# A one-core transformer block: in the gate and up projections, one 2x2 block of products per column chunk formed as seven products of sums

## The chip, the cores and the metric

The kernel runs on one core of a Trainium2 chip, in one launch, all in float32. The metric is device time in microseconds (us), the median of several runs. Matmuls run on TensorE (PE) and write to PSUM, which has eight banks of 128 partitions x 512 float32. VectorE (DVE) and ScalarE (ACT) do elementwise work, SyncE (SP) issues the weight loads, and semaphores order the engines.

## The reference

For 256 tokens and D = 2048 it computes a feed-forward layer, a mixer and a second feed-forward layer, each followed by a layer norm. The change touches the first two products of both feed-forward layers:

```python
def swiglu(x, w_gate, w_up, w_down):                  # D = 2048, D_FF = 5632
    return (jax.nn.silu(x @ w_gate) * (x @ w_up)) @ w_down

h = layer_norm(DEEPNORM_ALPHA * h + 0.5 * swiglu(h, ffn1_w_gate[l], ffn1_w_up[l], ffn1_w_down[l]), ...)
mix = hybrid_mixer(h, ...)
h = layer_norm(DEEPNORM_ALPHA * h + mix, ...)
h = layer_norm(DEEPNORM_ALPHA * h + 0.5 * swiglu(h, ffn2_w_gate[l], ffn2_w_up[l], ffn2_w_down[l]), ...)
```

## The kernel before

**Units.** Every weight matrix is streamed in units of 256 rows x 512 columns (512 KB): SP loads a unit into one of eight `raw` slots (L422). To keep float32 precision, each unit is split in two: ACT copies it to a rounded `whi` (`split_hi`, L486), DVE subtracts to get the rest, `wlo` (`split_lo`, L493). There are three split slots. The activations `xT` are kept as the same kind of pair. A product is then three matmuls (hi x hi, hi x lo, lo x hi; L505, L506, L507), each with a 128x128 block of `xT` as weights and 512 columns moving. A unit has two 128-row blocks and is used by two halves of the tokens (t0, t1), so it is 12 matmuls (`token_mm`, `unit_mm`).

**Chunks.** The 5632 gate and up columns are 11 chunks of 512. A chunk is 8 gate units, summed in the two banks `acc0`, and 8 up units, summed in the two banks `acc1`: 192 matmuls. Chunk 0 is written out by hand; chunks 1 to 10 are one loop on each engine (`gate_up` in `ffn_pe`, `ffn_act`, `ffn_dve`, `ffn_loads`). Within a chunk ACT takes tanh of the gate (L1079), DVE turns it into the gate's silu (L1184, `gated`) and, once all up units of the chunk are done, multiplies by `acc1` (`gate_times_up`, L977); PE transposes the result in the next chunk, after its fourth unit (`hT_pe`, L958, 8 small matmuls into `tp`), and ACT and DVE split it into `hT` (L964, L968).

**What sets the order.** All orders are written out by hand, per engine, and engines run their queues in order. Four counters carry the dependences: `raw_loaded` (a slot has landed), `hi_done`, `lo_done` (splits done) and `unit_used` (PE is through with a unit's split). ACT and DVE split `LEAD` = 2 units ahead of PE, so a `split_hi` waits for `unit_used` of the unit that had its slot. SP loads a slot again when `lo_done` says it was split. `Stream` and `ring_place` work out the counts and the slots.

**Seven products, already in use elsewhere.** The down projection (`Pair`, `form_mm`, L1026 to L1028) already computes some 2x2 blocks (two token halves x two units of rows, two column chunks) with seven products P1 to P7 instead of eight. It needs sums of weight blocks (DVE, L1203 to L1218, 128x1024 each), sums of activations (`sumA`), and foldings of the product banks.

Of the kernel before, what the change touches and what calls it, by code (L numbers as in the profile page):

```python
# [19 lines left out]
P = 128  # L20
# [16 lines left out]
class Phase:  # L37


    def __init__(self, name, iters, units, width, raws=None):  # L40
        self.name, self.iters, self.units, self.width = name, iters, units, width
        self.raws = units if raws is None else raws

    def places(self, slots):

        return self.raws if slots == RAW_SLOTS else self.units

# [96 lines left out]
class Stream:  # L144


    def __init__(self, phases):
        self.phases = phases
        self.base = []
        self.loads = []  # L150
        at, loads = 0, [0] * RAW_SLOTS
        for ph in phases:
            self.base.append(at)
            self.loads.append(list(loads))
            at += ph.iters * ph.units
            for s in range(RAW_SLOTS):
                loads[s] += ph.iters * self.uses(ph, s)

    @staticmethod
    def uses(ph, s):  # L160
        return sum(ring_place(u, ph.raws, RAW_SLOTS) == s for u in range(ph.raws))
# [5 lines left out]
    def loaded(self, p, it, u):  # L167

        n = self.phases[p].raws
# [6 lines left out]
    def freed(self, p, it, u, slots):  # L176
# [5 lines left out]
        s = ring_place(u, n, slots)  # L182
        same = [v for v in range(u) if ring_place(v, n, slots) == s]
        if same:
            c = same[-1] + 1
        else:
            prev = [v for v in range(n) if ring_place(v, n, slots) == s]
            c = prev[-1] - n + 1 if prev else -n
            if not over:
                if p > 0:  # L190
                    m = self.phases[p - 1].places(slots)
                    prev = [v for v in range(m) if ring_place(v, m, slots) == s]
# [7 lines left out]
def hybrid_block(nc, x, x_t, ffn1_w_gate, ffn1_w_up, ffn1_w_down, ln1_g, ln1_b, w_in, q_norm_g, kv_norm_g,  # L200
# [40 lines left out]
    F1GU, F1DA, F1DB, WA, WZ, WB, WC, WQI, WUQ, WO, F2GU, F2DA, F2DB = range(13)  # L241
    QI_CHUNKS, UQ_CHUNKS, QU = IH * ID // BANK, AH * AD // BANK, QT // UNIT_KT
    st = Stream([
        Phase("ffn1 gate and up", GATE_CHUNKS, 2 * KU, BANK),
        Phase("ffn1 down: chunks 0 and 1", 1, len(PAIRS[0].items), BANK, len(PAIRS[0].raws)),
        Phase("ffn1 down: chunks 2 and 3", 1, len(PAIRS[1].items), BANK, len(PAIRS[1].raws)),
# [7 lines left out]
        Phase("ffn2 gate and up", GATE_CHUNKS, 2 * KU, BANK),  # L254
        Phase("ffn2 down: chunks 0 and 1", 1, len(PAIRS[0].items), BANK, len(PAIRS[0].raws)),
        Phase("ffn2 down: chunks 2 and 3", 1, len(PAIRS[1].items), BANK, len(PAIRS[1].raws)),
# [9 lines left out]
    with ExitStack() as ctx:  # L266
# [23 lines left out]
        form_sum = mz("form_sum", 88, [P, UNIT_KT, BANK])  # L290
        fourth_hi = mz("fourth_hi", 92, [P, 1, UNIT_KT, BANK], F32R)
# [89 lines left out]
        pinv = at("pinv", cz + 1824, [P, T, AH])  # L381
        alog = at("alog", cz + 1888, [P, BH])
# [34 lines left out]
        def load_unit(sp, p, it, u, src):  # L417
            s = ring_place(u, st.phases[p].units, RAW_SLOTS)
# [10 lines left out]
        def split_place(p, it, u):  # L429

            n = st.phases[p].units
            if p in (F1DB, F2DB) and n - EDGES <= u < n:
                slot = u - n + EDGES
                return edge_hi, edge_lo, slot, st.index(p, 0, edge_free(slot))
            if plan_of(p) is not None:
# [4 lines left out]
                elif s < SPLIT_SLOTS:  # L440
                    last = [v for v in range(2 * KU) if ring_place(v, 2 * KU, SPLIT_SLOTS) == s][-1]
                    free = st.index(GU[f], GATE_CHUNKS - 1, last + 1)
# [30 lines left out]

        def raw_unit(p, u):
# [3 lines left out]
        def split_hi(act, p, it, u):  # L478
            n, w = st.phases[p].units, cut_width(p, it, u)
            hi, _, s, free = split_place(p, it, u)  # L480
            v = raw_unit(p, u)
            r = ring_place(v % st.phases[p].raws, n, RAW_SLOTS)
# [4 lines left out]

        def split_lo(dve, p, it, u):
            n, w = st.phases[p].units, cut_width(p, it, u)
            hi, lo, s, _ = split_place(p, it, u)  # L490
            r = ring_place(raw_unit(p, u) % st.phases[p].raws, n, RAW_SLOTS)
# [4 lines left out]
        def token_mm(pe, p, it, u, acc, half, stat, kt0, first, last):  # L496
# [4 lines left out]
            for k in range(UNIT_KT):  # L501
# [3 lines left out]
                pe.matmul(o, hi, w_hi[:, s, k, 0:width], start=first and k == 0, stop=False)  # L505
                pe.matmul(o, hi, w_lo[:, s, k, 0:width], start=False, stop=False)  # L506
                ins = pe.matmul(o, lo, w_hi[:, s, k, 0:width], start=False, stop=last and k == UNIT_KT - 1)  # L507
# [320 lines left out]
        GU, DOWN = [F1GU, F2GU], [(F1DA, F1DB), (F2DA, F2DB)]  # L828
        EXITS, ENTRIES = (F1DB, WO, F2DB), (WA, F2GU)
# [35 lines left out]
        def ffn_loads(sp, f, w_gate, w_up, w_down, load_x):  # L865
# [4 lines left out]
            def gate_up(c):  # L870
                for v, view in ((0, gate_v), (KU, up_v)):
                    for u in range(KU):
                        load_unit(sp, GU[f], c, v + u, view[:, 2 * u:2 * u + 2, bass.ds(c * BANK, BANK)])
# [8 lines left out]
            with sp.Fori(1, GATE_CHUNKS) as c:  # L882
                gate_up(c)
# [3 lines left out]
            for pair, p in enumerate(DOWN[f]):  # L887
                plan = PAIRS[pair]
                for r, (u, c) in enumerate(plan.raws):
                    s = ring_place(r, len(plan.raws), RAW_SLOTS)  # L890
                    if r < RAW_SLOTS and pair == 0:
                        sp.wait_ge(lo_done, st.freed(p, 0, r, RAW_SLOTS))
                    elif r < RAW_SLOTS:
                        before = max(v for v in range(len(PAIRS[0].raws)) if v % RAW_SLOTS == s)
# [21 lines left out]
        F_STEPS = len(SUM_STEPS) + sum(PAIR_STEPS)  # L916

        def summed(f, step):

            return F_STEPS * f + SUM_STEPS.index(step) + 1  # L920

        def made(f, p, name, q):

            pair = DOWN[f].index(p)
            return F_STEPS * f + len(SUM_STEPS) + sum(PAIR_STEPS[:pair]) + 4 * q + MADE[name]

        def folded(f, pair, n):

            return F_STEPS * f + len(SUM_STEPS) + sum(PAIR_STEPS[:pair]) + 4 * len(PAIRS[pair].quads) + n
# [5 lines left out]
        def sum_act(f, n):  # L935

            return 6 * f + n + 1

        def form_raw(p, i):
# [3 lines left out]
            return raw[:, plan_of(p).raw_of(i) % RAW_SLOTS]  # L943
# [1823 lines left out]
```

## Time and profile before

| | us |
|---|---|
| median of 3 runs | 1924.69 (1923.57 to 1925.12) |
| the profiled execution, its own time | 1924.74 |
| its span, first to last instruction | 1923.0 |
| PE busy | 1903.5 (99%) |
| DVE busy | 1256.1 (65%) |
| ACT busy | 893.1 (46%) |

The two gate and up stages lie at about 6 to 495 us and 1190 to 1680 us of the span, the two down stages behind them, the mixer between 725 and 1190 us. The span is what the trace covers; the time outside it is 1.7 us. "Busy" of PE counts matmuls whose ends are modelled and that overlap, so the spacing of their starts says more than their durations. A row of a timeline gives start, duration, engine, line and operation, and in brackets how long the engine had been idle and what released it.

### The profile page before, as it was taken

How to read it: one execution, taken by the hardware profiler on the slowest of the kernel's cores; microseconds unless marked ns; L12 is line 12 of the kernel's file. 1: busy time of each engine (PE TensorE's matmuls, PEld its weight loads, DVE VectorE, ACT ScalarE, POOL GpSimd, SP SyncE). 2: the span in 40 equal slices, each digit the busy share in tenths (PEclk: the TensorE clock that was granted, in tenths of full speed). 3: DMA queues.
4: the chain of work that ended last, by engine and by line, in shares of the span. 5: the costliest groups of instructions: out<-in, count | busy, mean ns of one | idle time of the engine just before them, and what ended most of it. 6: DMA issues, size and time to landing. Idle time of an engine off the chain costs nothing.

```text
span 1923.0 us, 28047 instructions
## 1 busy us (share of the span) xinstructions
PE 1903.5 (99%) x10490; PEld 1621.3 (84%) x10490; DVE 1256.1 (65%) x1415; ACT 893.1 (46%) x996; POOL 66.9 (3%) x93
## 2 busy tenths in 40 slices
PE   9999999999999999999999999999999999999997
PEld 7888888888888888999999888888888888888886
DVE  5555555455788887667766958554555555588887
ACT  5444444344454553554744534443444444455452
POOL 0000000000000001300131000000000000000000
PEclk9999999999999999999999999999999999999999
DMA  8666666667655575664442067566566666646654
GB/s 305 188 191 189 187 191 185 189 176 238 199 173 200 180 283 155 214 188 150 130 132 89 23 218 252 167 186 190 178 189 189 200 187 191 188 133 214 217 193 186
DMA packets 185366, 357.38 MB, mean 186 GB/s; under 512 B 11328, under 2 KB 23616, under 8 KB 184272
## 3 DMA queue, kind: packets, MB, share of 16 engines
q1 hardware_dynamic: 183600, 347.43, 57.9%
q0 software_dynamic: 1696, 8.99, 1.4%
q8 instruction: 47, 0.77, 0.2%
q14 instruction: 23, 0.19, 0.0%
HBM read 354.28 MB, written 2.10 MB: 185 GB/s over the span
## 4 chain that ended last, share of the span: by engine, by line
PE 90%; DVE 5%; DMA 2%; issue 1%; ACT 1%; POOL 0%; POOLq 0%; DVEq 0%; ACTq 0%
PE acc L505 24%; PE acc L507 24%; PE acc L506 24%; PE acc L528 3%; PE acc L532 3%; PE acc L530 3%; DMA raw<-in_ffn_w_down_dram 2%; PE tp L1026 1%; PE tp L1028 1%; PE tp L1027 1%; PE tp L958 1%; DVE wlo L493 1%; PE acc L1026 1%; PE acc L1028 1%; PE acc L1027 1%
## 5 line engine op out<-in xcount | busy, mean ns | idle before, releaser
L493 DVE TENSOR_TENSOR wlo<-raw,whi 128x1024 fp32r<-128x1024 f32 (+2 forms) x559 | 668.0, 1201 | 576.4 <-ACT whi L486 574.8
L486 ACT ACTIVATE whi<-raw 128x1024 fp32r<-128x1024 f32 (+2 forms) x559 | 575.1, 1036 | 746.2 <-PE acc L507 676.7
L505 PE MATMUL acc<-whi,xT 128*128 128x512 f32 (+2 forms) x1644 | 631.7, 384 | 0.8 <-ACT zab L1662 0.4
L507 PE MATMUL acc<-whi,xT 128*128 128x512 f32 (+2 forms) x1644 | 626.5, 381 | 0.0
L506 PE MATMUL acc<-wlo,xT 128*128 128x512 f32 (+2 forms) x1644 | 625.9, 381 | 0.0
L505 PEld LDWEIGHTS acc<-whi,xT 128*128 128x128 f32 x1644 | 309.0, 188 | 64.5 <-issue 1.8
L507 PEld LDWEIGHTS acc<-whi,xT 128*128 128x128 f32 x1644 | 308.9, 188 | 59.2
L506 PEld LDWEIGHTS acc<-wlo,xT 128*128 128x128 f32 x1644 | 309.1, 188 | 55.7
L505 PE MATMUL acc<-whi,hT 128*128 128x512 f32 x352 | 137.6, 391 | 1.1 <-DVE wlo L493 1.1
L507 PE MATMUL acc<-whi,hT 128*128 128x512 f32 x352 | 137.2, 390 | 0.0
L506 PE MATMUL acc<-wlo,hT 128*128 128x512 f32 x352 | 137.2, 390 | 0.0
L528 PE MATMUL acc<-xT,whi 128*128 128x256 f32 x384 | 108.9, 284 | 0.0
L532 PE MATMUL acc<-xT,wlo 128*128 128x256 f32 x384 | 108.9, 283 | 0.0
L530 PE MATMUL acc<-xT,whi 128*128 128x256 f32 x384 | 108.9, 283 | 0.0
L1098 ACT ACTIVATE whi<-raw 128x1024 fp32r<-128x1024 f32 x54 | 57.4, 1062 | 48.8 <-PE acc L507 16.5
L505 PEld LDWEIGHTS acc<-whi,hT 128*128 128x128 f32 x352 | 66.1, 188 | 15.7 <-issue 1.6
L507 PEld LDWEIGHTS acc<-whi,hT 128*128 128x128 f32 x352 | 66.1, 188 | 13.8
L506 PEld LDWEIGHTS acc<-wlo,hT 128*128 128x128 f32 x352 | 66.1, 188 | 13.6
L530 PEld LDWEIGHTS acc<-xT,whi 128*128 128x128 f32 x384 | 73.9, 192 | 0.0
L532 PEld LDWEIGHTS acc<-xT,wlo 128*128 128x128 f32 x384 | 73.8, 192 | 0.0
L528 PEld LDWEIGHTS acc<-xT,whi 128*128 128x128 f32 x384 | 73.8, 192 | 0.0
L1224 DVE TENSOR_TENSOR wlo<-raw,whi 128x1024 fp32r<-128x1024 f32 x54 | 65.9, 1221 | 4.9 <-ACT whi L1098 4.3
(382 smaller groups left out, 2046.1 us busy)
## 6 DMA issues: line engine op xcount, KB each, us to landing
raw<-in_ffn_w_down_dram SPq DMA_DIRECT2D x176, 512.0 KB, 6.7
raw<-in_ffn_w_up_dram SPq DMA_DIRECT2D x175, 512.0 KB, 3.7
raw<-in_ffn_w_gate_dram SPq DMA_DIRECT2D x174, 512.0 KB, 3.8
raw<-in_w_in_dram SPq DMA_DIRECT2D x48, 512.0 KB, 3.9
raw<-in_w_out_dram SPq DMA_DIRECT2D x32, 512.0 KB, 7.0
raw<-in_w_in_dram SPq DMA_DIRECT2D x32, 260.0 KB, 2.8
raw<-in_w_in_dram SPq DMA_DIRECT2D x16, 456.0 KB, 6.1
raw<-in_w_q_idx_dram SPq DMA_DIRECT2D x8, 512.0 KB, 4.0
```

The costliest lines, as they stand in the source:

```text
L486: act.activation(hi[:, s, :, 0:w], raw[:, r, :, 0:w], ACT.Copy).then_inc(hi_done, 1)
L493: dve.tensor_tensor(lo[:, s, :, 0:w], raw[:, r, :, 0:w], hi[:, s, :, 0:w].bitcast(F32), ALU.subtract).then_inc(lo_done, 1)
L505: pe.matmul(o, hi, w_hi[:, s, k, 0:width], start=first and k == 0, stop=False)
L506: pe.matmul(o, hi, w_lo[:, s, k, 0:width], start=False, stop=False)
L507: ins = pe.matmul(o, lo, w_hi[:, s, k, 0:width], start=False, stop=last and k == UNIT_KT - 1)
L528: pe.matmul(o, whi[:, s, k, cols], hi, start=first and k == 0 and c == 0, stop=False, skip_group_check=True)
L530: pe.matmul(o, whi[:, s, k, cols], lo, start=False, stop=False, skip_group_check=True)
L532: ins = pe.matmul(o, wlo[:, s, k, cols], hi, start=False, stop=end, skip_group_check=True)
L1026: pe.matmul(o, x_hi, w_hi[:, s, k], start=i == touches[0] and k == 0, stop=False)
L1027: pe.matmul(o, x_hi, w_lo[:, s, k], start=False, stop=False)
L1098: act.activation(w_hi[:, s], form_raw(p, i), ACT.Copy).then_inc(hi_done, 1)
L1224: dve.tensor_tensor(w_lo[:, s], form_raw(p, i), w_hi[:, s].bitcast(F32), ALU.subtract)\
```

## The change

The change gives each chunk 2 to 10 of both feed-forward layers one 2x2 block: token halves t0 and t1, row units 6 and 7 (`QUAD_A`, `QUAD_B`), and as its two columns the gate and the up weights of the chunk. With X the activations and G, U the weights, the eight unit-half products of units 6 and 7 (48 matmuls) become seven (42): P1 = X(t0,6) G6, P2 = X(t0,7) G7, and P3 to P7 with sums of weights (DVE, `chunk_add`) and sums of activations (`sumX`, made once per layer, in chunk 1).

P1, P5, P6 and P7 of a chunk are computed at the end of the chunk before it, P2, P3 and P4 at its start. Call g0 to g5 the plain gate units of a chunk and u0 to u5 its plain up units. The new order of a looped chunk c is: g0, P2, g1, P3, g2, P4, g3, g4, g5, u0, u1, then for chunk c+1 P1, u2, P5, P6, u3, P7, and u4, u5 of chunk c. P5 goes to the bank `tp[3]`, P7 to `tp[2]`, P6 and P1 to the halves of `acc0`. Foldings combine them: U2 = P1 + P6, U3 = U2 + P7 (into `acc0[1]`, where P4 and gate units are added), U4 = U2 + P5 (ACT copies it into `acc1[0]` as a seed for P3 and up units), V = U4 + P7 (into `acc1[1]`). Chunk 1 ("lead": 8 gate units and 2 up units, then the 10 items above from u0 on) and chunk 10 ("last", 15 items) are written out, chunks 2 to 9 are the loop. There are four split slots in the loop instead of three, and ACT and DVE run three items ahead (`CHUNK_LEAD`).

```diff
+def chunk_plans(a, b, units):
+    some = [u for u in range(units) if u not in (a, b)]
+    gate, up = plain(0, some), plain(1, some)
+    here = [gate[0], ("P2", 0, 0), gate[1], ("P3", 0, 0), gate[2], ("P4", 0, 0), *gate[3:]]
+    ahead = up[:2]
+    ahead += [("P1", 0, 0), up[2], ("P5", 0, 0), ("P6", 0, 0), up[3], ("P7", 0, 0), *up[4:]]
+    raws_here = [(some[0], 0, 0), (b, 0, 0)] + [(u, 0, 0) for u in some[1:]]
+    u1 = [(u, 1, 0) for u in some]
+    raws_ahead = u1[:2] + [(a, 0, 1), (a, 1, 1), u1[2], (b, 1, 1), *u1[3:]]
+    lead = plain(0, range(units)) + plain(1, (a, b)) + ahead
...
+    body, last = here + ahead, here + up
+    shift = len(here) - 1
...
+            Chunk(body, raws_here + raws_ahead, [(i + (i >= shift)) % 4 for i in range(len(body))]),
...
+        sumX = mz("sumX", 92, [P, 4, UNIT_KT, 2, P], F32R)
+        gate_sum = mz("gate_sum", 80, [P, UNIT_KT, BANK])
+        gate_sum2 = mz("gate_sum2", 84, [P, UNIT_KT, BANK])
...
+        folding = at("folding", cz + 1888, [P, BANK])
```

PE. A product is six matmuls; the waits in front of it:

```diff
+            def chunk_form(p, it, c, i):
...
+                if name in ("P1", "P6"):
+                    half = int(name == "P6")
+                    pe.wait_ge(acc0_free[half], c + (n0[GU[f]] + 1))
+                if name == "P5":
+                    pe.wait_ge(sem("formed"), in_gate(f, "S4 low") if p == G1[f] else in_chunk(f, p, it, "U4"))
+                if name == "P7" and p != G1[f]:
+                    pe.wait_ge(sem("formed"), in_chunk(f, p, it, "V"))
+                if name == "P3":
+                    pe.wait_ge(sem("sum_act"), act_in_chunk(f, p, it, "seed"))
+                pe.wait_ge(lo_done, st.index(p, it, i + 1))
```

SP. When a `raw` slot is free again, as the item whose `split_lo` must be done:

```diff
+            def released(plan, r):
+
+                u, c, ahead = plan.raws[r]
+                if u == QUAD_B and c == 0 and not ahead and ("P4", 0, 0) in plan.items:
+                    return plan.at("P4") - 1
+                if (u, c, ahead) == (QUAD_A, 0, 1):
+                    return plan.at("P1") + 1
+                if (u, c, ahead) == (QUAD_A, 1, 1):
+                    return plan.at("P7")
+                if (u, c, ahead) == (QUAD_B, 1, 1):
+                    return len(plan.items) + CHUNKS[1].at("P3")
+                return plan.at("unit", u, c)
```

ACT and DVE, the loop over a chunk's items:

```diff
+                for i in range(CHUNK_LEAD, n + (LEAD if p == GE[f] else CHUNK_LEAD)):
+                    if i == CHUNK_LEAD and p != G1[f]:
+                        act.wait_ge(sem("formed"), in_chunk(f, p, it, "U4"))
+                        act.wait_ge(acc1_free[0], c + n1[GU[f]])
+                        act.activation(acc1[:, 0], folding[:], ACT.Copy).then_inc(sem("sum_act"), 1)
+                    split_hi(act, p, it, i)
...
+                    if p != GE[f] and i == plan.at("P1") + 4:
...
+                        act.activation(folding[:], acc0[:, 0], ACT.Copy).then_inc(sem("sum_act"), 1)
...
+                gate_times_up(dve, f, c, st.index(p, it, 0))
+                if p != G1[f]:
+                    to_folding(p, it, "U4")
+                    second_up(p, it, c)
+                for i in range(CHUNK_LEAD, n + (LEAD if p == GE[f] else CHUNK_LEAD)):
+                    split_lo(dve, p, it, i)
+                    if p == G1[f]:
+                        x_sums(i)
                     if i == 8:
                         hT_dve(dve, f, c)
+                    if i + 2 < n and plan.items[i + 2][0] in ("P4", "P5", "P6", "P7"):
+                        chunk_add(p, it, plan.items[i + 2][0])
+                    if i == gate_end + 3:
+                        gate_part(c)
+                    if p != GE[f] and i == n:
+                        to_folding(p, it, "U2")
+                    if p != GE[f] and i == n + 1:
+                        to_folding(p, it, "U3")
```

How the order moves. VectorE, at the start of a looped chunk, from its first instruction on (`gated` x `acc1`), before:

```order
L977 TENSOR_TENSOR gated<-gated,acc 128x512 [waits s_acc0a_free,s_unit_used]
L977 TENSOR_TENSOR gated<-gated,acc 128x512 [waits s_acc0b_free]
L492 REGISTER_ALU
L493 TENSOR_TENSOR wlo<-raw,whi 128x1024 [waits s_hi_done]
L492 REGISTER_ALU
L493 TENSOR_TENSOR wlo<-raw,whi 128x1024 [waits s_hi_done]
```

The same place in the changed kernel, from behind those two multiplications (there L1212) on; `folding` holds U2, then U4, `tp` is P5 and then P7, `chunk_lo` is the fourth split slot, `gate_sum` and `gate_sum_62` are the two weight sums:

```order
L1550 TENSOR_TENSOR folding<-tp,folding 128x512 [waits s_formed]
L1554 REGISTER_ALU
L1556 TENSOR_TENSOR acc<-tp,folding 128x512 [waits s_acc1b_free,s_formed]
L1149 REGISTER_ALU
L1150 TENSOR_TENSOR chunk_lo_65<-raw,chunk_hi_64 128x1024 [waits s_hi_done]
L1507 ISA
L1532 REGISTER_ALU [waits s_raw_loaded4]
L1533 REGISTER_ALU [waits s_formed]
L1534 TENSOR_TENSOR gate_sum<-raw,gate_sum_62 128x1024 [waits s_lo_done]
L1149 REGISTER_ALU
L1150 TENSOR_TENSOR wlo<-raw,whi 128x1024 [waits s_hi_done]
```

Between the multiplications and the low split of g2 (the last row) stand U4, V, the low split for P3 and the weight sum for P4; before, the low splits followed the multiplications at once.

TensorE, where up units 5 and 6 met in the loop before; a unit is twelve matmuls, of which the last three and the first three are shown:

```order
L505 MATMUL acc<-whi,xT 128x512
L506 MATMUL acc<-wlo,xT 128x512
L507 MATMUL acc<-whi,xT 128x512
L515 REGISTER_ALU
L505 MATMUL acc<-whi,xT 128x512 [waits s_lo_done]
L506 MATMUL acc<-wlo,xT 128x512
L507 MATMUL acc<-whi,xT 128x512
```

And the end of u2, P5 and the first matmuls of P6 in the loop now:

```order
L631 MATMUL acc<-whi,xT 128x512
L1253 REGISTER_ALU
L1258 REGISTER_ALU [waits s_formed]
L1266 MATMUL tp<-whi,sumX 128x512 [waits s_lo_done]
L1267 MATMUL tp<-wlo,sumX 128x512
L1268 MATMUL tp<-whi,sumX 128x512
L1266 MATMUL tp<-whi,sumX 128x512
L1267 MATMUL tp<-wlo,sumX 128x512
L1268 MATMUL tp<-whi,sumX 128x512
L1258 REGISTER_ALU [waits s_acc0b_free]
L1266 MATMUL acc<-chunk_hi_64,sumX 128x512 [waits s_lo_done]
L1267 MATMUL acc<-chunk_lo_65,sumX 128x512
```

A product takes six matmuls between two waits for a split, where a unit takes twelve, and it has a second wait of its own.

## Rows read from the trace of the kernel before

**Rows 1.** The page: busy time and share of the span by engine; granted clock in tenths

```profile
PE 1903.5 (99%) x10490; PEld 1621.3 (84%) x10490; DVE 1256.1 (65%) x1415; ACT 893.1 (46%) x996; POOL 66.9 (3%) x93
PEclk9999999999999999999999999999999999999999
```

**Rows 2.** Waits: who waited for whom, us in total, times, longest

```profile
ACT whi L486 <- PE acc L507: 676.7, 385, 4.4
DVE wlo L493 <- ACT whi L486: 574.8, 396, 4.7
...
PE acc L505 <- DVE wlo L493: 1.1, 3, 0.4
```

**Rows 3.** Windows: start:end, length, busy and count by engine, clock, DMA share, GB/s

```profile
227.95:272.42 44.47, 44.47 (x201) 36.83 (x200) 23.01 (x21) 18.62 (x18) 0.00 (x0) 1.00 0.65 188
561.00:700.00 139.00, 139.00 (x614) 115.17 (x614) 120.17 (x111) 75.72 (x74) 0.43 (x1) 1.00 0.59 203
```

**Rows 4.** Timeline of TensorE over the start of a chunk, and its transposes

```profile
227.72 0.39 PE L507 MATMUL acc<-whi,xT 128*128 128x512 f32 x1
227.95 0.39 PE L505 MATMUL acc<-whi,xT 128*128 128x512 f32 x1
228.17 0.39 PE L506 MATMUL acc<-wlo,xT 128*128 128x512 f32 x1
228.40 0.39 PE L507 MATMUL acc<-whi,xT 128*128 128x512 f32 x1
228.63 0.39 PE L505 MATMUL acc<-whi,xT 128*128 128x512 f32 x1
...
238.83 1.04 PE L958 MATMUL tp<-ident,gated 128*128 128x128 f32 x8
239.63 0.47 PE L505 MATMUL acc<-whi,xT 128*128 128x512 f32 x1
```

**Rows 5.** Timeline of VectorE and ScalarE, same chunk

```profile
228.15 1.28 DVE L977 TENSOR_TENSOR gated<-gated,acc 128x512 f32<-128x512 f32 x2 [0.40 <-PE acc L507]
229.35 1.22 DVE L493 TENSOR_TENSOR wlo<-raw,whi 128x1024 fp32r<-128x1024 f32 x1
...
257.39 2.36 DVE L493 TENSOR_TENSOR wlo<-raw,whi 128x1024 fp32r<-128x1024 f32 x2 [1.91 <-ACT whi L486]
...
228.15 1.06 ACT L486 ACTIVATE whi<-raw 128x1024 fp32r<-128x1024 f32 x1 [1.66 <-PE acc L507]
```

**Rows 6.** Lines: groups by line, busy us and mean ns, idle before

```profile
L977 DVE TENSOR_TENSOR gated<-gated,acc 128x512 f32<-128x512 f32 x44 | 28.3, 684 | 9.7 <-PE acc L507 9.7
L1218 DVE TENSOR_TENSOR form_sum<-raw 128x1024 f32<-128x1024 f32 x14 | 17.1, 1220 | 0.0
L2151 DVE COPY t<-tp 128x256 f32<-128x256 f32 x10 | 4.1, 423 | 7.4 <-PE tp L2470 7.2
L840 ACT ACTIVATE whi<-raw 128x512 fp32r<-128x512 f32 x6 | 3.8, 632 | 1.1 <-DMA raw<-in_ffn_w_up_dram 0.9
```

**Rows 7.** DMA issues: size and median us to landing

```profile
raw<-in_ffn_w_down_dram SPq DMA_DIRECT2D x176, 512.0 KB, 6.7
raw<-in_ffn_w_up_dram SPq DMA_DIRECT2D x175, 512.0 KB, 3.7
raw<-in_w_out_dram SPq DMA_DIRECT2D x32, 512.0 KB, 7.0
```

**Rows 8.** Landing times of raw in 540:700 (down), then in 230:275 (gate and up)

```profile
DMA to landing us min/median/max: 3.7/7.5/15.4
...
DMA to landing us min/median/max: 3.6/3.7/4.8
```

**Rows 9.** Windows: TensorE busy, clock, DMA share, GB/s, opening and end of down

```profile
0.00:22.00 22.00, 19.68 (x90) 1.00 0.93 338
700.00:740.00 40.00, 38.95 (x184) 1.00 0.88 287
```

More of the change, by code:

```diff
@@ L181, in freed @@
             it, u = it + 1, u - n
-        s = ring_place(u, n, slots)
-        same = [v for v in range(u) if ring_place(v, n, slots) == s]
+        ph = self.phases[p]
+        s = ph.place(u, slots)
+        same = [v for v in range(u) if ph.place(v, slots) == s]
         if same:
@@ L186, in freed @@
         else:
-            prev = [v for v in range(n) if ring_place(v, n, slots) == s]
+            prev = [v for v in range(n) if ph.place(v, slots) == s]
             c = prev[-1] - n + 1 if prev else -n
@@ L253, in hybrid_block @@
         Phase("w_out", OUT_CHUNKS, KU, BANK),
[L254 to L256 removed]
+        *gate_up_phases("ffn2"),
+        *down_phases("ffn2"),
     ])
@@ L440, in split_place @@
                 elif s < SPLIT_SLOTS:
-                    last = [v for v in range(2 * KU) if ring_place(v, 2 * KU, SPLIT_SLOTS) == s][-1]
-                    free = st.index(GU[f], GATE_CHUNKS - 1, last + 1)
+                    last = [v for v, slot in enumerate(CHUNKS[2].slots) if slot == s][-1]
+                    free = st.index(GE[f], 0, last + 1)
                 else:
@@ L996, in ffn_pe, with chunk_unit @@
-            gate_up(0, False)
-            with pe.Fori(1, GATE_CHUNKS) as c:
-                gate_up(c, True)
+            if f == 0:
+                first_units_pe(pe)
+            else:
+                entry_units(pe, 2, F2GU)
+            def chunk_unit(p, it, c, i):
+                plan = chunk_of(p)
+                _, u, kind = plan.items[i]
+                mine = [v for v, item in enumerate(plan.items) if item[0] == "unit" and item[2] == kind]
+                quad = p != G1[f]
+                pe.wait_ge(lo_done, st.index(p, it, i + 1))
+                for half in range(2):
+                    first = i == mine[0]
+                    if first and not quad:
+                        pe.wait_ge((acc0_free, acc1_free)[kind][half], c + (n0, n1)[kind][GU[f]])
+                    elif first and kind == 0 and half == 0:
+                        pe.wait_ge(sem("sum_act"), act_before_chunk(f, p, it, "P1 out"))
+                    elif first and kind == 0:
+                        pe.wait_ge(sem("formed"), before_chunk(f, p, it, "U3"))
+                    elif first and half == 1:
+                        pe.wait_ge(sem("formed"), in_chunk(f, p, it, "V"))
+                    ins = token_mm(pe, p, it, i, (acc0, acc1)[kind], half, xT, 2 * u, first and not quad,
+                                   i == mine[-1], quad)
+                    if kind == 0 and half == 0 and i == mine[-1]:
+                        ins.then_inc(acc0a_done, 1)
+                ins.then_inc(unit_used, 1)
```

444 lines of the change are left out of this document (359 added, 85 removed).

## The prediction

> **What bounds the kernel now.** I read the page first: TensorE is busy 99% of the span and its granted clock is full in every slice; VectorE has 65%, ScalarE 46% [rows 1]. The waits say the same from the other side: the long ones are ScalarE waiting for TensorE to free a split slot (676.7 us) and VectorE waiting for ScalarE (574.8 us), while TensorE waits for a low split three times in the whole run, 1.1 us [rows 2]. So both helpers idle in front of TensorE, and a microsecond of matmuls taken out is a microsecond of time as long as the helpers still come first. Then the windows: one looped chunk of gate and up (227.95 to 272.42) takes 44.47 us, with TensorE busy throughout, VectorE 23.01 us and ScalarE 18.62 us [rows 3]. Last the timeline, for what one matmul is worth: the starts lie at 227.95, 228.17, 228.40, 228.63, which is 0.2267 us each, though each row lasts 0.39 because they overlap [rows 4]. 192 x 0.2267 = 43.53 us, and the transposes take the rest: 238.83 to 239.63 is 0.8 us, and some 0.14 more before the spacing is back, 44.47 in all.
>
> **TensorE's saving.** A chunk with a 2x2 block has 6 + 6 plain units (144 matmuls) and 7 products of six (42): 186 in place of 192. Its P1, P5, P6 and P7 are issued one chunk early, so the counts per chunk differ (216 in chunk 1, 186 in chunks 2 to 9, 162 in chunk 10), but the sum is what counts: 216 + 8 x 186 + 162 = 1866 against 10 x 192 = 1920. That is 54 fewer for each feed-forward layer, 108 in all, and 108 x 0.2267 = 24.5 us. The loads stay the same (16 units a chunk), and so does what follows.
>
> The Trainium skill (TensorE: Matmul & The Clock Gate, Back-to-back issue gap) gives N/2.4 + 2.5 ns for the gap of a matmul, 216 ns for 512 columns; by it the saving would be 23.3 us. The trace differs, with 0.2267 us; I go by the trace.
>
> **Products in place of units.** Is a product worth exactly six spacings? They go to other banks, with two waits ahead. The second window lies in the down projection, which already has such products: 614 matmuls in 139.00 us, 0.2264 each, TensorE busy for all of it [rows 3]. So nothing is added for them: 0, with a bound of 0.1 us each below.
>
> **VectorE's and ScalarE's load.** VectorE gets, per chunk, 3 more low splits (19 items instead of 16) and 4 weight sums, at 1.22 us each (the existing weight sums: 1220 ns), and 4 foldings of 512 columns at 0.68 (the multiplication's 684 ns) [rows 6]: 8.5 + 2.7 = 11.3 us, 34.3 in a chunk of 44.47 - 1.36 = 43.1 us, 80%. In the down window it has 120.17 of 139.00 us, 86%, and TensorE still doesn't wait [rows 3]. ScalarE gets 3 x 1.06 (its splits, [rows 5]) + 2 x 0.63 ([rows 6], the 128x512 split): 23.1 us, 54%. Neither becomes the bound; what remains is whether one piece comes too late.
>
> **The tightest place: the start of a chunk.** Let 0 be the chunk's first matmul. TensorE runs g0 to 2.72, P2 to 4.08, g1 to 6.80, P3 to 8.16, g2 to 10.88. VectorE may multiply when the last up unit is done: 228.15 - 227.95 = 0.20, and its next instruction starts at 1.40 (229.35) [rows 5]. Now U4 runs 1.40 to 2.08 and V 2.10 to 2.79. ScalarE waits for U4: the seed 2.15 to 2.78, the high split of P3 to 3.84. VectorE: low split of P3 from 3.87; behind it the sum for P4 and the low split of g2 follow at 1.14 apiece (two back to back take 2.36, so 1.14 + 1.22, [rows 5]): 5.01, 6.15, done at 7.37. TensorE wants P3's split at 6.80 (it is done at 5.09: 1.7 to spare) and g2's at 8.16: 0.8 us to spare. Queued behind V on VectorE is everything of that chunk, so it is the one place where all slips together. The further register and wait steps that the order shows there (7 between the multiplications and g2's split, where there were 2) have no price in the trace; each costs nothing if it runs under the instruction before it, and 0.1 us each (a guess from the 0.03 to 0.1 us that dependent pairs show) would still leave 0.1. I take 0.
>
> **The chunk's end.** Continued in the same way: the sums for P5 and P6 are made at about 23.5 and 27.1, behind tanh (which waits for g5, done at 21.4), and the low splits are ready at 28.3, 29.5 and, for P7, 33.4; TensorE wants them at 30.9, 32.3 and 36.4. P1 needs `acc0[0]` at 26.9, which VectorE frees at 24.1. U3 is made at 41.3, wanted at 44.5 (second half of g0). Two microseconds or more everywhere: side by side, P5 and P6 use up 2.7 us of split work against 2.7 us of matmuls, and the plain units around them give it back.
>
> **The loads.** SP issues in order, and two `raw` slots are now held long: the up unit 6 of the next chunk (its P7 is split at 33.4) and the up unit 7 (until P3's split, 5.1 of the next chunk). So the loads of g1 and g2 are issued at 33.4, and g3, g4, g5, u0, u1 in one burst at 5.1. A load lands after 3.7 us in gate and up [rows 7]. g1: 37.1, wanted by ScalarE at 40.7. g3: 8.8, its splits follow at 9.9 and 11.1, and TensorE wants it at 13.25 (10.88, transposes 1.0, P4 1.36): 2.15 us to spare. The rest of the burst at the 338 GB/s of the opening [rows 9] takes 1.55 us each and is used every 2.7 us. So nothing again.
>
> **Seams.** Chunks 0 to 1, 1 to 2, 9 to 10 and 10 to down are new hand-overs. Chunk 1 has besides 12 sums of activations of 256 columns on VectorE (12 x 0.42 = 5.1 us [rows 6], in a chunk of 49.9 us with some 32 us of other work). TensorE's waits for a low split were 1.1 us over three times, so four seams in each of two layers at 0 to 0.4 give 0 to 3.2 us. They can't be below nothing, since TensorE doesn't wait there today. I take 1.0.
>
> **Sum.** 1924.74 (the profiled execution; the median is 1924.69, so nothing to correct) - 24.5 + 1.0 = 1901.2 us.
>
> **Rivals.** (a) The chain at the chunk's start is late. For: 0.8 us of room under nine dependent steps; the walk uses the shortest hand-overs the trace shows. Against: the same kinds of steps in down cost 1.1 us in all. If they come 1.3 us later than worked out, TensorE stands for 0.5 us in each of 18 chunks: 9 us, 1910. All of the gain is gone only at 1.36 us a chunk.
> (b) The products cost TensorE something by themselves (a second wait each): 0.1 us x 7 x 18 = 12.6 us, 1914. Against it stands the spacing of 0.2264 in down.
> (c) Slower than before: the burst. The load of g3 is on a thread from P3's low split: issue, landing, two splits, TensorE. It decides from a landing time of 3.7 + 2.15 = 5.9 us, and from 5.9 + 1.36 = 7.2 the kernel is slower than before. In down, where SP also issues in bursts, loads land after a median of 7.5 us, up to 15.4, though 3.7 at best [rows 8]; w_out's 7.0 [rows 7]. At 7.5: 1.6 us x 18 = 29 us, 1929. Against: g3 is the first of its burst, and those before it (g1, g2) landed long ago; and the later ones have 2.7 us of room more for each place.
> The Trainium skill (TensorE: Matmul & The Clock Gate, Loop structure matters more than you think) adds that a TensorE that waits for loads between matmuls goes cold. The trace has no such case at this size: with 1.05 us idle in 700 to 740 the granted clock stayed 1.00 [rows 9], so I put no price on it for (a) to (c).
> (d) It doesn't do what it says, for instance because TensorE is held between chunks by `acc0[1]` or `acc1[0]`, now written by other engines in mid-use: near 1.4 us a chunk, 1925.
>
> **Chances and range.** Forecast (1900 to 1905) 0.74; (a) 0.10; (b) 0.05; (c) 0.06; (d) 0.05, half of it within 0.2%. A measurement of this kernel can tell about 0.2% (3.8 us) from no change. Faster 0.90, same 0.03, slower 0.07. The range: at the low end 1924.74 - 24.5 with no seam cost and 0.7 for the scatter of the runs, 1899.5; at the high end (a) and a little, 1911; what lies beyond is most of (b), (c) and (d).
>
> **What would show it.** Right: in a looped chunk 186 matmuls spaced 0.227 and a period of 43.1 us (first transpose to first transpose); VectorE near 34 us of it; ScalarE still waiting for TensorE; no row of TensorE waiting for a low split, `formed` or `sum_act` above some us in total. (a) would show as TensorE waiting for the low split of g2, once a chunk; (b) as gaps ahead of the `tp` products; (c) as ScalarE waiting for a gate load, and landing times above 6 us for it; (d) as waits on ScalarE's seed or on `acc`. A period above 43.6 us, or a wait in every chunk, makes the prediction wrong, and so does a total of matmuls that is not 108 lower.

## The result, and the profile after

| | before | after |
|---|---|---|
| median, us (4 runs each, same chip) | 1924.38 | 1897.94 (1897.59 to 1899.05) |
| profiled execution / its span, us | 1924.74 / 1923.0 | 1897.59 / 1895.9 |
| matmuls | 10490 | 10382 |
| one looped chunk, transpose to transpose, us | 44.48 | 43.07 |

The ratio is 0.9864 (95% interval 0.9847 to 0.9881): 26.4 us faster. The forecast was 1901.2 with a range from 1899.5. The direction, the mechanism and nearly all of the size came out, and the time lies 3.3 us below the forecast and 1.6 us below the range. A second measurement of the same kernel, beside the last runs of the experiments, gave 1897.46 (1896.93 to 1897.97).

The page after, same lines as [rows 1]:

```profile
PE 1878.3 (99%) x10382; PEld 1602.0 (84%) x10382; DVE 1450.9 (77%) x1637; ACT 970.4 (51%) x1094; POOL 66.9 (4%) x93
PEclk9999999999999999999999999999999999999999
```

TensorE is still the bound, at the full granted clock (its level of 2.4 GHz) in every slice. VectorE went from 65% to 77% of the span. The waits, against [rows 2]:

```profile
ACT whi L1143 <- PE acc L631: 157.8, 124, 2.6
DVE wlo L1150 <- ACT whi L1143: 145.2, 133, 2.8
ACT acc L1381 <- DVE folding L1550: 65.7, 18, 3.7
ACT whi L1143 <- DMA raw<-in_ffn_w_gate_dram: 43.6, 24, 3.1
PE acc L3179 <- POOL ident L3149: 1.5, 1, 1.5
PE acc L629 <- DVE wlo L617: 1.0, 3, 0.4
```

The helpers still wait for TensorE. TensorE's own waits for a low split are three, 1.0 us, as before, and none lies in a chunk. The third and fourth rows are new: ScalarE waits 18 times for U4, ahead of its seed, and 24 times for a gate load, the first of the burst among them. Neither reaches TensorE. The window of one looped chunk (length, then busy and count of TensorE, its weight loads, VectorE, ScalarE, GpSimd; clock, DMA share, GB/s), against [rows 3]:

```profile
240.06:283.14 43.08, 43.08 (x195) 35.74 (x194) 32.80 (x33) 22.04 (x24) 0.00 (x0) 1.00 0.55 192
```

TensorE fills the chunk; VectorE has 32.80 us of it (34.3 worked out) and ScalarE 22.04 (23.1). The working added up whole durations, while busy time counts only once the ends at which two rows overlap. The timeline of VectorE at a chunk's start, where the prediction saw the tightest place; TensorE's first matmul of this chunk starts at 229.18:

```profile
229.38 1.28 DVE L1212 TENSOR_TENSOR gated<-gated,acc 128x512 f32<-128x512 f32 x2 [0.40 <-PE acc L631]
230.58 0.68 DVE L1550 TENSOR_TENSOR folding<-tp,folding 128x512 f32<-128x512 f32 x1
231.30 0.70 DVE L1556 TENSOR_TENSOR acc<-tp,folding 128x512 f32<-128x512 f32 x1
232.91 1.23 DVE L1150 TENSOR_TENSOR chunk_lo<-raw,chunk_hi 128x1024 fp32r<-128x1024 f32 x1 [0.92 <-ACT chunk_hi L1143]
234.06 1.22 DVE L1534 TENSOR_TENSOR gate_sum<-raw,gate_sum 128x1024 f32<-128x1024 f32 x1
235.19 1.22 DVE L1150 TENSOR_TENSOR wlo<-raw,whi 128x1024 fp32r<-128x1024 f32 x1
```

Counted from 229.18: U4 at 1.40 (1.40 forecast), V at 2.12 (2.10), the low split of P3 at 3.73 (3.87), the sum for P4 at 4.88 (5.01), the low split of g2 from 6.01 to 7.23 (6.15 to 7.37). TensorE wants it at 8.16: 0.93 us of room where 0.8 was worked out. This chunk is of the first layer. Read in the same way in all 18 chunks, the room is 0.93 us in the first layer's, 0.76 in the second layer's, and 0.59 in the last chunk of either layer, so 0.59 is the least. The load of g3 stands in SP's row and ScalarE's:

```profile
234.30 1.61 SPq L1028 DMA_DIRECT2D raw<-in_ffn_w_gate_dram  x3
```

```profile
237.92 1.06 ACT L1143 ACTIVATE whi<-raw 128x1024 fp32r<-128x1024 f32 x1 [1.47 <-DMA raw<-in_ffn_w_gate_dram]
```

Issued at 5.12 (5.1 forecast), split at 8.74; the landing was put at 8.8. The landing times of `raw` in 240 to 284, against [rows 8], are longer than before, and more than half of them lie past the 5.9 us from which rival (c) was to count. That bound was for g3 alone, and no load is late enough for TensorE to wait; ScalarE's split of g3 started 3.62 us after the issue:

```profile
DMA to landing us min/median/max: 3.4/6.3/9.7
```

**Where the 3.3 us are.** Cut at the starts of TensorE's matmuls, the two profiled executions divide so (us); the opening, the 31.2 us of layer 2's entry and the end behind the last matmul, alike in both within 0.12, are left out:

| stage | before | after | less | 54 matmuls explain |
|---|---|---|---|---|
| chunk 0, layer 1 | 43.80 | 43.84 | 0.0 | |
| chunks 1 to 10, layer 1 | 444.83 | 432.06 | 12.77 | 12.24 |
| down, layer 1 | 229.71 | 228.76 | 0.95 | |
| from there to the end of w_out | 459.57 | 458.89 | 0.68 | |
| gate and up, layer 2 | 464.06 | 451.31 | 12.75 | 12.24 |
| down, layer 2 | 232.45 | 232.24 | 0.2 | |

The fourth and the last row can't be told from scatter: in the runs below, all alike there, the fourth lies at 458.79 to 459.47 and the last at 231.55 to 233.43. Only the fourth row's 459.57 of before lies outside, by 0.1. The first row's 0.0 is one pair too: chunk 0 takes 43.80 to 44.58 us in the four kernels that keep the order of before and 43.83 to 44.08 in the others. Left over the matmuls are 0.53 + 0.51 us in gate and up and 0.95 us in the first down stage. Sections 1 to 3 of the experiments look for these, 4 and 5 at the room that the change leaves.

### The profile page after: what moved, and what is told of

Same layout as the page of the kernel before. It is cut to its first block, busy times and chain, and to the rows that moved or that the text cites. A ratio compares the mean times of both kernels' runs of the same rounds, so it can differ in the third digit from the quotient of the medians.

```text
span 1895.9 us, 28391 instructions
## 1 busy us (share of the span) xinstructions
PE 1878.3 (99%) x10382; PEld 1602.0 (84%) x10382; DVE 1450.9 (77%) x1637; ACT 970.4 (51%) x1094; POOL 66.9 (4%) x93
## 4 chain that ended last, share of the span: by engine, by line
PE 94%; DVE 4%; issue 1%; DMA 1%; ACT 1%; POOL 0%; POOLq 0%; DVEq 0%; ACTq 0%
PE acc L629 21%; PE acc L631 21%; PE acc L630 21%; PE acc L653 3%; PE acc L657 3%; PE acc L655 3%; PE acc L1268 2%; PE acc L1266 2%; PE acc L1267 2%; PE tp L1312 1%; PE tp L1310 1%; PE tp L1311 1%; PE tp L1193 1%; PE tp L1268 1%; PE tp L1267 1%; PE tp L1266 1%
## 5 line engine op out<-in xcount | busy, mean ns | idle before, releaser
L629 PE MATMUL acc<-whi,xT 128*128 128x512 f32 (+2 forms) x1132 | 429.5, 379 | 0.8 <-ACT zab L2107 0.4
L631 PE MATMUL acc<-whi,xT 128*128 128x512 f32 (+2 forms) x1132 | 426.2, 377 | 0.0
L630 PE MATMUL acc<-wlo,xT 128*128 128x512 f32 (+2 forms) x1132 | 425.9, 376 | 0.0
L1150 DVE TENSOR_TENSOR wlo<-raw,whi 128x1024 fp32r<-128x1024 f32 x248 | 303.2, 1222 | 146.0 <-ACT whi L1143 143.4
L617 DVE TENSOR_TENSOR wlo<-raw,whi 128x1024 fp32r<-128x1024 f32 (+2 forms) x239 | 277.9, 1170 | 154.3 <-ACT whi L601 152.9
L1143 ACT ACTIVATE whi<-raw 128x1024 fp32r<-128x1024 f32 x248 | 262.5, 1059 | 222.9 <-PE acc L631 139.3
L601 ACT ACTIVATE whi<-raw 128x1024 fp32r<-128x1024 f32 (+2 forms) x239 | 238.1, 1005 | 227.6 <-PE acc L631 159.8
L629 PEld LDWEIGHTS acc<-whi,xT 128*128 128x128 f32 x1132 | 212.6, 188 | 42.2 <-issue 1.7
L631 PEld LDWEIGHTS acc<-whi,xT 128*128 128x128 f32 x1132 | 212.6, 188 | 38.5
L630 PEld LDWEIGHTS acc<-wlo,xT 128*128 128x128 f32 x1132 | 212.7, 188 | 38.0
L1150 DVE TENSOR_TENSOR chunk_lo<-raw,chunk_hi 128x1024 fp32r<-128x1024 f32 x72 | 88.2, 1225 | 43.1 <-ACT chunk_hi L1143 40.0
L631 PE MATMUL acc<-chunk_hi,xT 128*128 128x512 f32 x224 | 87.1, 389 | 0.0
L629 PE MATMUL acc<-chunk_hi,xT 128*128 128x512 f32 x224 | 87.1, 389 | 0.0
L1415 ACT ACTIVATE whi<-raw 128x1024 fp32r<-128x1024 f32 x54 | 57.4, 1062 | 46.8 <-PE acc L631 16.3
```

The source lines that it names most:

```text
L601: act.activation(hi[:, s, :, 0:w], raw[:, r, :, 0:w], ACT.Copy).then_inc(hi_done, 1)
L617: dve.tensor_tensor(lo[:, s, :, 0:w], raw[:, r, :, 0:w], hi[:, s, :, 0:w].bitcast(F32), ALU.subtract).then_inc(lo_done, 1)
L1143: act.activation(hi[:, s], src, ACT.Copy).then_inc(hi_done, 1)
L1150: dve.tensor_tensor(lo[:, s], src, hi[:, s].bitcast(F32), ALU.subtract).then_inc(lo_done, 1)
L1415: act.activation(w_hi[:, s], form_raw(p, i), ACT.Copy).then_inc(hi_done, 1)
```

## Experiments

**1. The end of the first down stage.** The diff has a part that the prediction read and gave no price: the ring of `raw` slots runs on from the first to the second pair of a down stage (`DOWN_RING + len(PAIRS[0].raws)`). Before, SP and TensorE at that exit, where the layer norm's transposes wait for `resid`:

```profile
708.97 18.38 SPq L422 DMA_DIRECT2D raw<-in_w_in_dram  x12
...
724.55 0.63 PE L616 MATMUL tp<-ident,resid 128*128 128x128 f32 x4 [0.81 <-DVE resid L781]
```

```profile
718.40 1.06 ACT L486 ACTIVATE whi<-raw 128x1024 fp32r<-128x1024 f32 x1 [1.39 <-DMA raw<-in_w_in_dram]
719.49 1.23 DVE L493 TENSOR_TENSOR wlo<-raw,whi 128x1024 fp32r<-128x1024 f32 x1 [1.22 <-ACT whi L486]
720.63 0.68 DVE L1289 SCALAR_TENSOR_TENSOR resid<-acc,resid 128x512 f32<-128x512 f32 x1
```

After:

```profile
686.70 25.69 SPq L511 DMA_DIRECT2D raw<-in_w_in_dram  x12
...
710.92 0.60 PE L741 MATMUL tp<-ident,resid 128*128 128x128 f32 x4
```

Before, the loads of `w_in` went out at 708.97, 15.6 us ahead of the transposes; ScalarE waited for one, VectorE for ScalarE's split of it, and `resid` stood behind that on VectorE, so TensorE waited 0.81 us. Now the loads go out 24.2 us ahead, and the transposes follow the last matmul by 0.233 us. Two runs take that part alone, one out of the changed kernel and one into the kernel before:

```
-        Phase(ffn + " down: chunks 2 and 3", ..., len(PAIRS[1].raws), DOWN_RING + len(PAIRS[0].raws))]
+        Phase(ffn + " down: chunks 2 and 3", ..., len(PAIRS[1].raws))]
...
-                        before = len(PAIRS[0].raws) - RAW_SLOTS + r
+                        before = max(v for v in range(len(PAIRS[0].raws)) if v % RAW_SLOTS == s)
```

> The changed kernel, with the down projection's loads put back to the raw slots that they had before: each of its two stages starts again at slot 0, where the change lets the ring of eight slots run on through both. Theory A: the 1.0 us by which the changed kernel leaves the first feed-forward layer earlier than the removed matmuls explain comes from this ring, because the loads of w_in no longer queue behind the last four loads of down. Then the first transposes behind the layer norm wait again some 0.9 to 1.2 us for VectorE (in the changed kernel the spacing there is 0.23 us), the first w_in load is issued about 9 us later than in the changed kernel, and the end comes about 1.0 us later, 1899 us, which the median can hardly tell. Rival B: the 1.0 us is the scatter of load landing times from one execution to the next; then the wait is as often there as not, and the issue time of the first w_in load stays.

Measured (e1): 1898.22 us (1897.63 to 1898.32), ratio 0.986 (0.9844 to 0.9877). The wait is back, though shorter:

```profile
696.28 18.04 SPq L510 DMA_DIRECT2D raw<-in_w_in_dram  x12
...
711.53 0.63 PE L740 MATMUL tp<-ident,resid 128*128 128x128 f32 x4 [0.48 <-DVE resid L905]
```

The spacing ahead of the transposes is 0.867 us, the stage 229.38 us against 228.76: 0.6 us, not the 0.9 to 1.2 expected. The interval of the time alone wouldn't have told it.

```
-        Phase("ffn1 down: chunks 2 and 3", 1, len(PAIRS[1].items), BANK, len(PAIRS[1].raws)),
+        Phase("ffn1 down: chunks 2 and 3", 1, len(PAIRS[1].items), BANK, len(PAIRS[1].raws), len(PAIRS[0].raws)),
...
-                        before = max(v for v in range(len(PAIRS[0].raws)) if v % RAW_SLOTS == s)
+                        before = len(PAIRS[0].raws) - RAW_SLOTS + r
```

> The kernel before, with only the ring of raw slots running on through the two down stages. Theory A: the wait of 0.8 us (1.2 us spacing) of the first transposes behind the first layer norm is gone, the first w_in load is issued some 9 us earlier, and the time is about 1.0 us lower, 1923.4 us. Rival B (scatter): the wait is where it was or moves by chance.

Measured (b1): 1923.88 us (1923.36 to 1924.62) beside 1924.87, ratio 0.9995 (0.9986 to 1.0005): not told apart by time, but by the trace:

```profile
700.82 25.61 SPq L433 DMA_DIRECT2D raw<-in_w_in_dram  x12
...
724.16 0.60 PE L632 MATMUL tp<-ident,resid 128*128 128x128 f32 x4
```

No wait, a spacing of 0.232 us, and the stage takes 228.73 us in place of 229.71. So the ring explains the first down stage, in both directions. The other traces agree: the three kernels with the old ring (before, e1 and b2 of section 3) take 229.38 to 229.71 us there and wait, the nine with the new one 228.71 to 228.76 us and don't. Rival B, chance, falls.

**2. The matmuls' own worth.** Here the changed kernel issues P7's six matmuls twice, so that a chunk has 192 again.

```
-                for k in range(UNIT_KT):
+                for k in [*range(UNIT_KT)] * (2 if name == "P7" else 1):
```

> The changed kernel, with the six matmuls of P7 issued twice (the second time they start the bank anew, so the result stays). Theory: the gain is the count of matmuls and nothing else, at 0.2267 us each; 6 x 18 = 108 more give 24.5 us back, 1922.4 us, period of a looped chunk 44.43 us. Rival 1: part of the gain came from better hand-overs in the chunk; then the time stays well below that of the kernel before, at 1920 or less even after correcting for the scatter. Rival 2: products cost more than six spacings by themselves; then it is above 1925.

Measured (e7): 1921.69 us (1921.24 to 1922.69), ratio 0.9984 (0.9975 to 0.9994). The chain of waits gives its period by the transposes of two chunks, and that of before:

```profile
245.54 0.87 PE tp L1193 x8
...
289.98 0.87 PE tp L1193 x8
```

```profile
239.00 0.87 PE tp L958 x8
...
283.49 0.87 PE tp L958 x8
```

44.44 against 44.49; over 15 looped chunks 44.43 against 44.48. Equal matmuls, and the new order is 0.05 us a chunk faster, so something in the old one cost TensorE that much. Against the changed kernel, from which this run differs in the 108 matmuls alone, chunks 1 to 10 of either layer take 444.30 us in place of 432.06: 12.24 us each, and 54 x 0.2267 is 12.24.

**3. What cost it.** Over the looped chunks of before, the mean spacing of matmuls at two places is not 0.227: where up units 1 and 3 begin it is 0.2305, 0.2395, 0.2325 and 0.2309. One instance, on ScalarE, VectorE and TensorE:

```profile
250.83 1.06 ACT L486 ACTIVATE whi<-raw 128x1024 fp32r<-128x1024 f32 x1 [4.38 <-PE acc L507]
```

```profile
251.93 1.23 DVE L493 TENSOR_TENSOR wlo<-raw,whi 128x1024 fp32r<-128x1024 f32 x1 [4.21 <-ACT whi L486]
253.07 1.28 DVE L1184 SCALAR_TENSOR_TENSOR gated<-gated,acc 128x512 f32<-128x512 f32 x2
```

```profile
253.36 0.40 PE L505 MATMUL acc<-whi,xT 128*128 128x512 f32 x1
253.60 0.40 PE L506 MATMUL acc<-wlo,xT 128*128 128x512 f32 x1
```

The low split ends at 253.16 and its first matmul starts at 253.36, on time but for 0.004 us: the split has only 0.20 us to spare, at both places and in every looped chunk. The cause is the ring: 16 units in 3 split slots don't come out even, `ring_place` slips twice a chunk, and there the split slot comes free one unit late. The changed kernel has 19 items in 4 slots and slips once, without harm. No view puts a wait down to it; only the starts show it. This run gives the kernel before the fourth split slot and nothing else:

```
+            if p in GU and (not isinstance(it, int) or u >= n):
+                v = u % n % 4
+                if isinstance(it, int):
+                    free = st.freed(p, it, u, SPLIT_SLOTS)
+                else:
+                    free = st.index(p, it, u - 2 if u % n == 2 else u - 3)
+                return (whi, wlo, v, free) if v < SPLIT_SLOTS else (fourth_hi, fourth_lo, 0, free)
```

> The kernel before, with a fourth split slot in the looped gate and up chunks (in the room that the down projection uses for its own fourth), so that 16 units fit the slots evenly; still two units of lead, and all 192 matmuls. Theory: with three slots the ring slips at up units 1 and 3 of each chunk, their splits become ready only as TensorE arrives, and the matmul starts there are spaced 231 to 239 ns instead of 227; 0.053 us a chunk. With four slots these are gone: period 44.43 us (44.483 before), 1.0 us less in all, 1923.9 us. Rival: the wider spacing comes from VectorE and ScalarE reading acc0 at that time; then it stays, since these reads stay where they are, and so does the period of 44.483.

Measured (b2): 1923.62 us (1922.23 to 1924.31) beside 1924.48, ratio 0.9993 (0.9984 to 1.0002); chunks 444.30 and 463.55 us, where before has 444.83 and 464.06; period 44.43. The interval of the time includes no change; the chunks' length and the period tell it. The same place, ScalarE, VectorE and TensorE:

```profile
251.14 1.03 ACT L1086 ACTIVATE gated<-acc 128x1024 f32<-128x1024 f32 x1 [4.38 <-PE acc L514]
252.06 1.05 ACT L493 ACTIVATE whi<-raw 128x1024 fp32r<-128x1024 f32 x1
```

```profile
252.20 1.29 DVE L1191 SCALAR_TENSOR_TENSOR gated<-gated,acc 128x512 f32<-128x512 f32 x2 [4.18 <-ACT gated L1086]
```

```profile
253.66 0.39 PE L512 MATMUL acc<-whi,xT 128*128 128x512 f32 x1
253.89 0.39 PE L513 MATMUL acc<-wlo,xT 128*128 128x512 f32 x1
```

The wide spacings are gone, at both places. The rival was that ScalarE's and VectorE's reading of `acc0` disturbs TensorE. The reads didn't stay where they were, as the expectation had it: counted from the chunk's transposes, ScalarE's comes 1.0 and VectorE's 1.2 us earlier here. The rival falls all the same: TensorE's spacing is 0.2267 us under both reads in this run, and at up unit 3 of the kernel before nothing reads `acc0` while the spacings are wide. With the ring as well (the edits of both runs together):

> The kernel before, with both the fourth split slot in the gate and up chunks and the ring of raw slots running on through down, and no product left out. Theory: together with the 108 matmuls (24.5 us) these two make up the change. So this kernel is at the time of the changed one with P7 issued twice (1921.7), 2 us below the kernel before: about 1922.8 with the 1.0 and 1.0 that the traces show, and the changed kernel is 24.5 us below it. Rival: there is a third cause; then it stays above 1923.5.

Measured (b3): 1922.79 us (1921.8 to 1923.08), ratio 0.999 (0.9981 to 0.9999), period 44.43, no wait at the exit. By the medians it is 1.69 us below the kernel before, where the traces' 1.04 and 0.95 make 1.99. The changed kernel, run beside it:

> The changed kernel again, beside the two above on one chip, as the other end of the sum: 1897.9 us.

Measured (a0): 1897.46 us (1896.93 to 1897.97), ratio 0.986 (0.9845 to 0.9875), span 1895.2. The two differ by 25.33 us in their medians. In the chunk stages they differ by 12.24 + 12.24 us, and 108 x 0.2267 is 24.48: the block products are worth their matmuls. The other 0.85 us lie outside the chunk stages, where the traces differ by a few tenths each way. The isolated gap that the Trainium skill gives for 512 columns (TensorE: Matmul & The Clock Gate, Back-to-back issue gap) would make that 23.3; these two runs don't agree with it.

**4. How much room the chunk's start has.** Between U4 and V, VectorE gets extra instructions that nothing uses, two of them or four:

```
+                dve.bn_stats(kstats[:, 0], folding[:])
+                dve.bn_stats(kstats[:, 1], folding[:])
+                dve.bn_stats(stats[:, 0, 0], folding[:])    # the run with four
+                dve.bn_stats(stats[:, 1, 0], folding[:])
                 dve.tensor_tensor(acc1[:, 1], tp[:, 2], folding[:], ALU.add)
```

> The changed kernel, with two more VectorE instructions (bn_stats over 512 columns, 0.7 us each, results unused) between U4 and V at each chunk's start, chunks 2 to 10. Theory: the chain there has 0.92 us of idle VectorE time ahead of P3's low split and 0.93 us of room behind g2's, 1.85 in all, so 1.4 us more change nothing: 1898 us, TensorE with no wait in the chunks, g2's low split done about 0.5 us ahead of its matmuls. Rival: the room is the 0.8 us of the prediction's walk; then each of 18 chunks loses 0.6 us, 1909 us.

Measured (e3): 1897.52 us (1897.11 to 1898.05), ratio 0.9858 (0.9841 to 0.9874), period 43.07, no wait. Counted from the chunk's start, V moved by 1.2 us, but the low split of g2 hardly did (its room is 0.76 us in the first layer's looped chunks and 0.58 in the second's):

```profile
232.41 0.68 DVE L1558 TENSOR_TENSOR acc<-tp,folding 128x512 f32<-128x512 f32 x1
233.00 1.22 DVE L1150 TENSOR_TENSOR chunk_lo<-raw,chunk_hi 128x1024 fp32r<-128x1024 f32 x1
...
235.27 1.22 DVE L1150 TENSOR_TENSOR wlo<-raw,whi 128x1024 fp32r<-128x1024 f32 x1
```

VectorE had been waiting 0.92 us for ScalarE's split behind V (the fourth row of its timeline above). The prediction's room ran from the split; V alone has that idle time more.

> The same with four more VectorE instructions, 2.8 us. Theory: 1.85 us of it is room, the other 0.95 us make TensorE wait for g2's low split once in each of 18 chunks: 17 us, 1915 us. Rival: the wait grows over the chunk, because VectorE is at 82% and doesn't catch up; then more than 25 us.

Measured (e4): 1910.64 us (1909.99 to 1911.69), ratio 0.9928 (0.9911 to 0.9945), period 43.785. Its VectorE, TensorE, and the waits:

```profile
235.17 0.68 DVE L1559 BATCH_NORM_STATS2 stats<-folding 128x6 f32<-128x512 f32 x1
235.76 0.68 DVE L1560 TENSOR_TENSOR acc<-tp,folding 128x512 f32<-128x512 f32 x1
...
238.62 1.22 DVE L1150 TENSOR_TENSOR wlo<-raw,whi 128x1024 fp32r<-128x1024 f32 x1
```

```profile
239.89 0.50 PE L629 MATMUL acc<-whi,xT 128*128 128x512 f32 x1 [0.32 <-DVE wlo L1150]
```

```profile
PE acc L629 <- DVE wlo L1150: 7.2, 18, 0.5
```

The wait comes where rival (a) put it, once in each of 18 chunks. The expected 1915 took 0.7 us for each extra instruction; they start 0.60 apart, so the four add 2.4 us. Over 15 looped chunks the split ends 0.51 us after the matmul was due (0.43 in the first layer, 0.60 in the second). The spacing there is 0.790 us in the mean and the next one 0.338, and the period grew by 0.715: 18 x 0.715 = 12.9, and 12.7 was measured.

**5. The other choices of the change.** P7 at the very end of the chunk:

```
-    ahead += [..., up[3], ("P7", 0, 0), *up[4:]]
+    ahead += [..., up[3], *up[4:], ("P7", 0, 0)]
```

> The changed kernel, with the two plain up units u4 and u5 ahead of P7 instead of behind it, so that the chunk ends with P7. Theory: U3 waits for P7, so it and the low split behind it move past the chunk's end, into the chain in front of P3 and g2: 0.69 + 1.14 us more, and the splits are not ahead any more. P3's split comes 0.3 us late and g2's 1.2 us late in all, 18 times: about 20 us, 1918 us, which is most of the gain. Rival: the chain has room enough (see the longer chains); then 1898 us, and the place of P7 is worth nothing.

Measured (e5): 1917.69 us (1916.58 to 1919.29), ratio 0.9966 (0.9953 to 0.9978), period 44.195. And high splits two items ahead in place of three:

```
-    CHUNK_LEAD = 3
+    CHUNK_LEAD = 2
```

> The changed kernel, with ACT and DVE two items ahead of TensorE instead of three. Theory: g1's splits now stand behind the multiplications, U4, V and the seed at the chunk's start; its low split is done at 4.97 us where TensorE wants it at 4.08, so 0.9 us in each of 18 chunks: 16 us, 1914 us, with TensorE waiting for the low split of g1. Rival: the third item of lead is not needed, since two were enough before; 1898 us.

Measured (e2): 1918.1 us (1916.97 to 1918.84), ratio 0.9966 (0.9953 to 0.9978), period 44.225. TensorE's waits in the two runs, and a matmul of the second:

```profile
PE acc L629 <- DVE wlo L1150: 10.9, 18, 0.6
```

```profile
PE acc L629 <- DVE wlo L1150: 15.3, 18, 0.9
```

```profile
237.62 0.50 PE L629 MATMUL acc<-whi,xT 128*128 128x512 f32 x1 [0.77 <-DVE wlo L1150]
```

Each gives back most of the saving, by one listed wait in a chunk. In the first run the split of g2 comes 0.73 us late, not 1.2. P3's split, expected 0.3 us late, comes 0.02 us early in the first layer and 0.06 late in the second; no wait is listed for it, but its two spacings are 0.31 and 0.34, which is another 0.2 us a chunk. The forecast of 1918 came out by errors that cancel. The wait of the second was expected rightly, its price not: the split ends 0.96 us late in the mean, and the period grew from 43.07 to 44.225, by 1.155. Here as in the run with four instructions, a late split cost its lateness and 0.2 us more, and the waits list less than either. The starts show where the 0.2 us go: the matmul starts 0.054 us after the split ends, the next spacing is 0.337 in place of 0.227, and a few behind it are wider by some thousandths. The Trainium skill (TensorE: Matmul & The Clock Gate, Loop structure matters more than you think) warns of a TensorE that goes cold when a long wait for a load stands between its matmuls. With these short waits for a split the granted clock stayed full in all 40 slices, and the spacings were back at 0.2267 within the chunk, so the extra price here is not the clock.

## Why the prediction was right, and where it failed

- **TensorE bounds it; the saving of 24.5 us.** Right: 108 fewer matmuls, and 24.48 us in the chunk stages between the changed kernel and the run that issues P7 twice, which differ in them alone. The period was put at 43.1 and is 43.07.
- **Products in place of units, at nothing.** Right: b3 and a0 differ in the chunks by 24.48 us, where 0.1 us a product would have made that 11.9. Rival (b) falls. The spacing of 0.2264 in down, with which the prediction argued, is a miscount: 614 matmuls touch the 139.00 us, but 613 start in it, and their spacing is 0.2267 as in gate and up. That is what "nothing is added" needs.
- **The tightest place.** Right within 0.14 us at each step, in the chunk shown; in the last chunk of a layer the room is 0.59 us, less than the 0.8 worked out. Rival (a) is a real mechanism: the run with four extra instructions and the two of section 5 bring about a late split in that chain; the order of the change escapes it by 0.59 to 0.93 us. The end of the chunk was right too: the low splits of P5, P6 and P7 are ready at 28.0, 29.3 and 33.4, where the prediction has 28.3, 29.5 and 33.4.
- **The burst.** Right: TensorE doesn't wait for a load in any chunk; g3 came at 8.74 where 8.8 was said. Rivals (c) and (d) don't occur. (Their prices, 1929 and 1925, leave out the 1.0 us of the seams that the forecast has; no chance hangs on it.)
- **"Seams. ... They can't be below nothing, since TensorE doesn't wait there today. I take 1.0."** This step failed. The new hand-overs cost nothing: the three listed waits are still 1.0 us in all, and chunks 1 to 10 with P7 issued twice take 444.30 us, the same as the kernel before with four split slots, which has none of them. And the floor was wrong: that no view lists a wait doesn't mean that no time is lost. The old hand-over at up units 1 and 3 lost 0.05 us a chunk to a split ready just in time, and the change's fourth slot gave 1.04 us back over both layers. The spacings of section 3, e7 and b2 show it.
- **"The loads stay the same (16 units a chunk), and so does what follows."** The loads do, but what follows doesn't. The diff also lets the ring of `raw` slots run on through down, and the wait of 0.81 us ahead of the layer norm's transposes, which stands in the trace of before, went: 0.95 us. I had read that line and looked for its effect in the chunks alone.
- **The low end.** It assumed the saving of matmuls as the most that could be gained, with 0.7 for scatter. The error of 3.3 us is 1.0 (seams counted, none there) + 1.04 + 0.95 + some 0.3. The last is where the sum started: at 1924.74, while the median of before over its four runs is 1924.38. The traces show no cause for it, and it is of the size of the scatter.

What stays open: why a split that is ready just in time stretches the next few spacings (0.2305, 0.2395, 0.2325, 0.2309), and why the last rows of the table vary by a few tenths between kernels that are alike there.

## What to carry to other kernels

Where TensorE is the bound, price a saving by the spacing of matmul starts in the trace, and the rest by walking the tightest chain step by step; the first held here to a few hundredths of a microsecond, the second to 0.14 us in the chunk shown, though the room then differed by up to 0.3 us from chunk to chunk. But don't take the absence of a listed wait for a floor of zero: compare the spacings right behind each hand-over with the mean, and where units and slots don't divide, expect a slip. Give each hunk of a diff its own term, in every stage whose ring, slots or order it touches, those after the stage it is meant for included.

## What the runs showed of the hardware

- A split that ends 0.20 us ahead of its first matmul costs about 0.026 us: spacings of 0.2305, 0.2395, 0.2325, 0.2309 in place of 0.227, with no wait listed. One that ended 0.58 us ahead (the run with two extra instructions) cost nothing.
- A late split costs TensorE its lateness and 0.2 us more: 0.51 us late was 0.715 a chunk, 0.96 us late was 1.155. The matmul starts 0.054 us after the split's end, and the next spacing is 0.337. The listed waits (0.4 in the mean and 0.5 at most, 0.85 and 0.9) are shorter than both, since the row of a matmul lasts longer than its spacing.
- Independent VectorE instructions overlap at their ends: 512 columns take 0.68 us but start 0.60 apart, 1024 columns 1.22 but 1.14 apart. A chain is to be summed by starts.
- A matmul of 512 columns is worth 0.2267 us, with weights loaded for each, in gate and up and in down alike.
